# Attention of a two-layer diffusion block: VectorE takes five low parts of weight panels one head pair later, and ScalarE copies the transposed probabilities ahead of the exponentials of context pairs

## What is computed

```python
N_HEADS, N_KV_HEADS, HEAD_DIM, GROUP = 16, 4, 64, 4
SEQ = CTX_LEN = 256; Q_BLOCK = 128

def _attend(q, k, v):
    s = jnp.einsum('bqhgd,bkhd->bhgqk', q * HEAD_DIM ** -0.5, k).astype(jnp.float32)
    p = jax.nn.softmax(s, axis=-1).astype(v.dtype)
    return jnp.einsum('bhgqk,bkhd->bqhgd', p, v)

k_all = jnp.concatenate([kc, kl], axis=1)      # latent queries see context and latent keys
v_all = jnp.concatenate([vc, vl], axis=1)
att_l = _attention_blocked(ql, k_all, v_all)
if not last:                                   # context queries see context keys alone
    att_c = _attend(_group(qc), kc, vc)
```

## Time and profile before

| | |
|---|---|
| median of three runs | 3099.43 us (3098.85 to 3101.8) |
| the profiled execution's own time | 3099.29 us |
| its span in the trace | 3097.5 us |
| TensorE busy | 3003.2 us, 97% of the span |
| weight loads of TensorE | 2488.3 us, 80% |
| VectorE busy | 2023.5 us, 65% |
| ScalarE busy | 1429.8 us, 46% |
| GpSimd busy | 190.7 us, 6% |
| mean granted TensorE clock | 0.998 of full speed |
| attention's pair loop, layer 0 | from about 996 to 1105 us of the span |
| attention's pair loop, layer 1 | from about 2648 to 2723 us |

### The profile page before, as it was taken

One profiled execution on the slowest core, in us unless ns is written; L12 is line 12 of the kernel. 1 busy time (PEld: TensorE's weight loads), 2 busy tenths in 40 slices (PEclk: granted clock), 3 DMA queues, 4 the chain that ended last, 5 costly groups with the idle time before them and its releaser, 6 DMA issues.

```text
span 3097.5 us, 49996 instructions
## 1 busy us (share of the span) xinstructions
PE 3003.2 (97%) x17660; PEld 2488.3 (80%) x17660; DVE 2023.5 (65%) x3710; ACT 1429.8 (46%) x2318; POOL 190.7 (6%) x152
## 2 busy tenths in 40 slices
PE   7999999999999999999999999999999999899998
PEld 5888877777887678888888888888877779699887
DVE  4776767777634744435665765757788776666777
ACT  4222366666445632234222342224676666644654
POOL 0000011212000000000000100001111010000000
PEclk9999999999999999999999999999999999999999
DMA  7544421111122022233443533533111114145454
GB/s 275 190 174 167 175 76 51 56 50 54 49 99 72 22 89 95 96 108 105 169 163 136 184 135 143 190 136 143 63 54 66 54 56 150 49 150 177 164 189 150
DMA packets 101843, 365.61 MB, mean 118 GB/s; under 512 B 11216, under 2 KB 12880, under 8 KB 101584
## 3 DMA queue, kind: packets, MB, share of 16 engines
q1 hardware_dynamic: 98384, 353.02, 32.0%
q10 hardware_dynamic: 3328, 10.81, 1.0%
HBM read 362.67 MB, written 1.11 MB: 117 GB/s over the span
## 4 chain that ended last, share of the span: by engine, by line
PE 83%; DVE 7%; ACT 5%; issue 4%; DMA 1%; SPq 0%; DVEq 0%; ACTq 0%; POOL 0%; POOLq 0%
PE bank L2025 64%; PE bank L2004 4%; DVE wlo L1234 2%; PE bank L2006 2%; PE bank L2356 1%; PE bank L2296 1%; ACT whi L542 1%; PE bank L2322 1%; PE bank L2298 1%; PE bank L2562 1%; PE bank L2390 1%; ACT ada_raw L884 1%; PE bank L2535 1%; ACT gc_row L1087 1%; ACT scr L1115 1%
## 5 line engine op out<-in xcount | busy, mean ns | idle before, releaser
L2025 PE MATMUL bank<-uh,whi 128*128 128x512 f32 (+1 forms) x2688 | 1016.3, 378 | 8.9 <-DVE wlo L1234 2.4
L542 ACT ACTIVATE whi<-raw 128x1024 fp32r<-128x1024 f32 x520 | 546.7, 1057 | 995.7 <-PE bank L2025 967.8
L2025 PE MATMUL bank<-uh,wlo 128*128 128x512 f32 (+1 forms) x2688 | 975.2, 363 | 0.5 <-DVE scr L1703 0.3
L2025 PE MATMUL bank<-ul,whi 128*128 128x512 f32 (+1 forms) x2688 | 975.1, 363 | 0.0
L1234 DVE TENSOR_TENSOR wlo<-raw,whi 128x1024 fp32r<-128x1024 f32 x520 | 637.6, 1227 | 383.6 <-ACT whi L542 376.1
L2025 PEld LDWEIGHTS bank<-uh,whi 128*128 128x128 f32 x2688 | 508.8, 189 | 100.5 <-issue 27.5
L2025 PEld LDWEIGHTS bank<-uh,wlo 128*128 128x128 f32 x2688 | 508.2, 189 | 79.1 <-issue 6.2
L2025 PEld LDWEIGHTS bank<-ul,whi 128*128 128x128 f32 x2688 | 509.5, 190 | 68.0 <-issue 6.3
L2025 PE MATMUL bank<-bh,whi 128*128 128x512 f32 (+1 forms) x930 | 340.1, 366 | 0.8 <-DVE bl L1942 0.8
L2025 PE MATMUL bank<-bl,whi 128*128 128x512 f32 (+1 forms) x930 | 337.6, 363 | 0.0
L2025 PE MATMUL bank<-bh,wlo 128*128 128x512 f32 (+1 forms) x930 | 337.6, 363 | 0.0
(11 more groups left out here) (304 smaller groups left out, 3766.3 us busy)
## 6 DMA issues: line engine op xcount, KB each, us to landing
raw<-stream SPq DMA_DIRECT2D x524, 512.0 KB, 3.2
ada_raw<-stream SPq DMA_DIRECT2D x131, 512.0 KB, 4.2
gc_row<-gc_rows ACTq DMA_DIRECT2D x16, 512.0 KB, 3.6
h<-h_in SPq DMA_DIRECT2D x1, 2048.0 KB, 10.7
m<-stream SPq DMA_DIRECT2D x4, 512.0 KB, 12.4
cst<-consts SPq DMA_DIRECT2D x1, 1104.0 KB, 13.4
scr<-stream SPq DMA_DIRECT2D x2, 512.0 KB, 16.2
lmat<-cond ACTq DMA_DIRECT2D x2, 512.0 KB, 4.0
```

What stands on the lines that cost most here:

```text
L542: act.activation(whi[:, j, :], raw[:, j, :], ACT.Copy).then_inc(hi_ready, 1)
L2025: last = mm(bank[j if to is None else to][:, c0:c1], w(t, a), x[:, t, c0:c1], start=n == 0, stop=n == 3 * kts - 1)
```

## The change

Two edits. In ScalarE's loop `evac_pt(n - 1)` stands ahead of the exponentials of pair n where n is a context pair other than pair 0; at all other pairs it stays behind them. That is seven pairs of layer 0 (3, 6, 9, 12, 15, 18, 21) and none of layer 1. In VectorE's loop the table of splits is read for n - 1: the low parts are made at the end of pairs 2, 3, 8, 14, 20 of layer 0 and 2, 3, 6, 10, 14 of layer 1. ScalarE's splits stay where they are. No instruction is added or removed.

```diff
@@ -1105,6 +1105,9 @@
 
                 gate_raw(0)
                 for n, (j, kind) in enumerate(pairs):
+                    early = n > 0 and kind == 0
+                    if early:
+                        evac_pt(n - 1)
                     for a in range(2):
                         act.wait_ge(A["s_max"], 2 * (n0 + n) + a + 1)
                         if n >= 2:
@@ -1123,7 +1126,8 @@
                     else:
                         if n > per and n % per == 1:
                             gate_raw(1 + n // per)
-                        evac_pt(n - 1)
+                        if not early:
+                            evac_pt(n - 1)
                     if n in splits:
                         split(*splits[n])
                 evac_pt(N - 1)
@@ -1857,8 +1861,8 @@
                         last.then_inc(A["s_scaled"], 1)
                         if a == 0:
                             out_low(n - 2)
-                    if n in splits:
-                        split(*splits[n])
+                    if n - 1 in splits:
+                        split(*splits[n - 1])
                 dve.sem_inc(pair_done[1], 3)
                 out_low(N - 2)
                 out_low(N - 1)
```

## The result

| | before | with the change |
|---|---|---|
| median of 12 runs | 3099.41 us (3097.53 to 3102.18) | 3107.06 us (3104.71 to 3110.24) |
| ratio, 95% interval | | 1.0024 (1.0017 to 1.0032) |
| profiled execution, own time / span | 3099.29 / 3097.5 us | 3104.71 / 3102.9 us |
| mean granted clock | 0.998 | 0.995 |
| `pv(0)` starts, layer 0 | 1001.15 us | 1003.13 us |

The change makes the kernel 7.65 us slower by the medians, 0.25%, with an interval of 0.17% to 0.32%. The last two rows hold the two loops that the change touches: layer 0 pays 11.8 us, layer 1 gives back 7.6, 4.2 us together. Where the rest comes from is taken up further down.

A forecast was written before the change was run, and what follows sets the result against it. TensorE was taken to set the pace, with some waits for ScalarE's copies. Waits netted +1.0 us, the fall gone -1.6, four new falls +6.4: +5.8 on 3099.29, so 3105.1 us, range 3098.5 to 3110.0.

The forecast's parts named there:

- within 0.2%: Whole kernel: time changes by less than 0.2% (6.2 us) either way; chance 0.55, made of 0.38 + 0.17.
- Part 1: Low parts one pair later: waits of 6.15 us go in layer 0, net 6.0 us in layer 1.
- The 0.3 us taken for pair 13's low part: Layer 1: this low part delays pair 15's maxima; 0.3 us of its 1.14 comes through, between 0 and 1.1.
- The claims on what hides the moved low parts: VectorE would wait for scores behind pair 8 anyway; DMAs 4.3 us later cost nothing, panels being wanted some 35 us later.
- Part 2: Layer 0, copies ahead of exponentials: `pv` waits 1.18 us at 9, 15, 21, 2.42 at 6, 12, 18, 2.32 at 3; 13.1 us.
- the link of 5.43 us: Layer 0: from context pair n's exponentials through scaling, maxima and exponentials of n+1 to n's copies, within a chain of 8.16 us.
- The two bounds: Layer 0, early copies' summed waits: 9.6 us if the chain overlaps better, 16 us at most; 13.1 taken.
- the spare 0.9: Layer 0, regular round: `pv(5)` could start at 1024.6, TensorE reaches it at 1025.5, so 0.9 us to spare.
- The clock: Falls at 1.6 us each: one gone in layer 1 (-1.6), four new behind layer 0's long waits (+6.4; ends 0 and 11.2).
- The first: Rival: layer 0's waits come as worked out but the clock holds or falls once; 3098.7 to 3100.3 us, chance 0.17.
- the third: Rival: layer 0's early copies don't hold the exponentials up, so they cost nothing; 3085.5 us, chance 0.04.
- The second: Rival: slower by over 0.2%, waits of 1.2 us growing past 1.6 or another gap drawing further falls; chance 0.41.

The follow-up runs named there:

- the version with the gate panel behind: Against the kernel before: low parts one pair later, no early copies, gate panel copied behind the transposes' copies; 3090.22 us (0.9966), repeated 3089.04 us (0.9964).

## Why the prediction was right, and where it was off

**Forecast and measurement.** 3105.1 us was forecast, 3107.06 measured, inside the range; the shift was +5.8 forecast, +7.65 measured. Part of this nearness is luck: the two pair loops, which are all that the forecast added up, moved by 4.15 us in the trace, and the rest came from outside them. The share that I gave to "within 0.2%", 0.55, was more than that of the slower side, 0.41, and the measurement fell on the slower side, by little.

**Part 1, the low parts.** Right. Layer 0: the run with this part alone gained 4.93 us, and 6.15 less the three waits of 0.40 which stay without the early copies is 4.95. Layer 1: 7.62 us, forecast 6.0 and the fall of 1.6. The 0.3 us taken for pair 13's low part measured 0.26, at `pv(14)`. The claims on what hides the moved low parts held: VectorE took the one of pair 7 between the scaling and the maxima of pair 9 in the low-parts-alone run, no wait of TensorE followed, and no split of ScalarE after the loop waited for a DMA (its idle time ahead of the thirteen splits behind the loop of layer 0 is 41.0 us in the traces before and with the change, all released by TensorE).

**Part 2, the early copies.** Right in place and size. Waits forecast 1.18, 2.42 and 2.32, measured 1.21, 2.45 and 2.36; sum 13.1 forecast, 13.36 measured. The trust in the link of 5.43 us, taken in one piece, was sound (6.00 measured with the gate panel's 0.57 in it). The two bounds are not what their words give: 2.8 less the spare 0.9 is 1.9 us, already above the forecast wait of 1.18. The 9.6 is 13.1 less seven times 0.5, and 16 comes out only as seven times 1.9 with the gate panels and the low part added. Of the 2.8 us by which the exponentials came late, 1.6 were taken up on the way to `pv` at pairs 9, 15 and 21; the spare 0.9 us of the copies do not tell that, the sum of the links does. The runs with the copies between the heads, with the gate panel behind and with the one low part moved took out one link each, and each wait shrank by that link.

**The clock.** This is the term of the sum that was mis-sized. Forecast was a fall behind all four long waits, 6.4 us; the profiled execution had three, 4.6 us, at 1.51 to 1.56 each. The missing 1.8 us were in part made good by 1.25 us from outside the loops, for which the forecast had no term. From the terms of the trace the profiled execution is explained: layer 0 +11.77, layer 1 -7.62, start of the loop +1.98, between the loops -0.67, after them -0.06: +5.40 us, and its own time differs by 5.42. It was the fastest of the twelve runs with the change, though, and the median is 2.3 us above it. A fourth fall (1.6) would explain most of that; unprofiled executions carry no trace, so this stays open.

**The page's rule on the clock.** The Trainium skill, TensorE: Matmul & The Clock Gate, under HAM oscillation, has longer gaps than these as the cause. By it there would have been no fall and 3098.7 us. The granted clock of 0.69 to 0.76 behind three waits of 2.3 to 2.4 us goes against it, and the measurement decides.

**The rivals.** The first (no fall, 3098.7) and the third (copies harmless) are ruled out, the third by the copies alone at 3111.08 us. The second, slower by more than 0.2%, is what the ratio shows, but not by its mechanism in the trace: no fifth fall, and no wait of 1.2 us grew past 1.6. The profiled execution, at +5.4 us, is still on the near side of the line of 6.2; the median is past it by what the trace of the fastest execution can't show.

**Where the expected gain went.** The change made the kernel 0.25% slower, while its parts alone moved the time by -0.34% and +0.41%. One part took waits out of both layers; the other put longer ones into layer 0, and the clock enlarged them.

## What to carry to other kernels

An operation that waits for a late producer should not stand ahead of work that is ready on an engine that runs in order, even if its own consumer is the bottleneck: work out when the consumer wants it (here the copies had 0.9 us to spare) and price what is queued behind (here it starts 2.8 us late, and 1.2 us of that reach TensorE at the plainest places). Moving an operation later on a side engine is free where the next thing on that engine waits for the bottleneck anyway, and dear where it falls into a chain, as the same low part did at `pv(3)`. A table of waits by place, each with its links, gave the waits of eight variants to within 0.2 us at each place, except for the three that falls of the clock covered in the run with the copies alone. The number of falls it did not give. Medians of whole runs could not have told the nearer ones apart.

## What the runs showed of the hardware that was not expected

**Behind long waits the clock fell often, but not always.** Behind waits of 2.3 to 2.4 us TensorE fell to its lower level in 11 of 14 cases over five kernels (3 of 4, 3 of 3, 1 of 3, 3 of 3, 1 of 1); behind 1.80 us in 1 of 3; behind 1.36 to 1.60 us in 1 of 7, the one of the earlier trace rows, and in none of 24 more at `pv(0)`; behind 1.15 us never. The same code had a fall in one trace and none in the other: `pv(2)` of layer 1 waited 1.60 us before the change and 1.59 us in the run with the copies alone, and only the first had a fall behind it.

**The clock fell without a wait, too.** Near 428 us, and again at one place between 2174 and 2194 us, TensorE works through 24 small matmuls, 8 and 16 columns wide. The traces show no idle time of it there, nor in the 6 us ahead of each fall, and the clock fell within 1.2 us behind them in 6 and in 8 of the 12 traces, as in the rows with the gate panel behind above: busy 5.00 of 5 us, granted clock 0.83.

**A fall can cover a wait.** At `pv(7)`, `pv(13)` and `pv(19)` of the run with the copies alone the waits of 0.82 us had vanished behind the falls of 1.6 us, so the two losses don't add.

**The start of the kernel varies more than most of the edits are worth.** In a stretch that no edit touches, `pv(0)` of layer 0 came between 1000.67 and 1005.38 us over the traces. The granted clock shows part of it. The kernel before, then the first run with the low parts alone:

```profile
35.00:40.00 5.00, 5.00 (x17) 4.07 (x17) 4.93 (x10) 4.89 (x8) 0.00 (x0) 0.72 1.02 407
...
430.00:435.00 5.00, 5.00 (x24) 4.08 (x23) 3.75 (x19) 4.91 (x7) 0.00 (x0) 1.00 0.26 90
```

```profile
35.00:40.00 5.00, 5.00 (x14) 4.10 (x15) 4.36 (x9) 4.64 (x7) 0.00 (x0) 0.50 1.02 408
...
430.00:435.00 5.00, 5.00 (x18) 4.00 (x18) 2.12 (x6) 3.42 (x7) 0.00 (x0) 0.66 0.32 108
```

Near 35 us the DMA engines are full (share 1.02) and TensorE waits for first weights; how long the clock stays low there differs from run to run, and near 430 us a fall comes in some traces and not in others. That is worth up to 4.7 us, so differences below some 2 us between medians of five runs say little in this kernel (an estimate; the medians of the low parts alone and of the version with the gate panel behind changed their distance from 1.97 to 0.39 us from one group of runs to the next).
